# Dilated attention's output gate: SiLU made from Tanh on ScalarE and a product on VectorE

## The reference, cut to what matters

```python
def dilated_layer(x, c, kv_groups, ada_w, ada_b, norm_g, w_in, q_norm_g, w_out):
    h = rms_norm(x, norm_g) * (1 + scale) + shift
    qz = h @ w_in                                  # 3 x 8 query heads and z, 8 x 128 wide
    q = rms_norm(q, q_norm_g) * (HEAD_DIM ** -0.5)
    ...
    alpha = jax.nn.softmax(jnp.stack(lses), axis=0)
    o = jnp.sum(alpha[..., None] * jnp.stack(outs), axis=0).astype(x.dtype)
    y = o.reshape(bsz, s, B_WIDTH) * jax.nn.silu(z)
    return x + gate * (y @ w_out)
```

## Time and profile before

| | |
|---|---|
| median of 3 runs | 2087.05 us (2085.76 to 2090.64) |
| profiled execution | 2079.87 us |
| its span, first to last instruction | 2078.2 us |
| TensorE busy | 1920.6 us, 92% |
| VectorE busy | 1135.0 us, 55% |
| ScalarE busy | 777.8 us, 37% |
| mean granted TensorE clock | 0.965 of full speed |
| stage qz | about 518 to 826 us |

### The profile page before, as it was taken

The page is one execution under the profiler, slowest core; times in us unless marked ns, Lnnn a source line. Parts: engine busy times, 40 slices in busy tenths (PEclk is TensorE's granted clock), DMA queues, the critical chain, the costliest instruction groups (busy, mean ns, idle before and its releaser), DMA issues.

```text
span 2078.2 us, 23372 instructions
## 1 busy us (share of the span) xinstructions
PE 1920.6 (92%) x8572; PEld 1542.5 (74%) x8572; DVE 1135.0 (55%) x1554; ACT 777.8 (37%) x999; POOL 39.3 (2%) x96
## 2 busy tenths in 40 slices
PE   5999999989999996999999987999996979999997
PEld 4788888867788884778888864776654758888885
DVE  6346565477366665554334556598645464433455
ACT  3455553243455554322323233224344342222232
POOL 1000000000000000000000000000000000000000
PEclk8999999989999998999999998999998999999997
DMA  8445655412222210233233241241211223334321
GB/s 306 154 122 176 179 169 158 136 61 81 61 61 61 61 61 21 81 101 96 78 110 101 71 111 41 86 116 42 61 41 52 90 58 85 90 91 121 87 73 63
DMA packets 288194, 198.41 MB, mean 95 GB/s; under 512 B 6562, under 2 KB 275188, under 8 KB 287092
## 3 DMA queue, kind: packets, MB, share of 16 engines
q1 hardware_dynamic: 279568, 163.63, 27.4%
q0 software_dynamic: 8064, 33.56, 4.6%
q10 hardware_dynamic: 484, 0.16, 0.0%
HBM read 195.21 MB, written 2.11 MB: 95 GB/s over the span
## 4 chain that ended last, share of the span: by engine, by line
PE 84%; DVE 8%; ACT 3%; issue 3%; DMA 1%; DVEq 0%; POOL 0%; ACTq 0%; POOLq 0%
PE acc L575 20%; PE acc L577 20%; PE acc L576 20%; PE acc L765 3%; PE acc L767 3%; PE acc L766 3%; PE acc L989 1%; DVE s_rstd L1497 1%; DMA s_ada_w<-in_a_ada_w 1%; PE ob L815 1%; PE acc L991 1%; PE acc L990 1%; ACT s_w_high L1047 1%; PE ob L831 1%; PE sc L949 1%
## 5 line engine op out<-in xcount | busy, mean ns | idle before, releaser
L1459 DVE TENSOR_TENSOR s_w_low<-s_raw,s_w_high 128x2048 fp32r<-128x2048 f32 x159 | 364.5, 2292 | 351.9 <-ACT s_w_high L1047 351.8
L575 PE MATMUL acc<-s_h_high,s_w_high 128*128 128x512 f32 x1248 | 494.4, 396 | 31.6 <-DVE s_h_low L1860 11.7
L576 PE MATMUL acc<-s_h_low,s_w_high 128*128 128x512 f32 x1248 | 487.7, 391 | 0.0
L577 PE MATMUL acc<-s_h_high,s_w_low 128*128 128x512 f32 x1248 | 487.5, 391 | 0.0
L1047 ACT ACTIVATE s_w_high<-s_raw 128x2048 fp32r<-128x2048 f32 x159 | 303.0, 1906 | 23.8 <-PE sc L660 17.9
L575 PEld LDWEIGHTS acc<-s_h_high,s_w_high 128*128 128x128 f32 x1248 | 235.3, 189 | 89.9 <-issue 35.7
L575 PE MATMUL acc<-s_b_high,s_w_high 128*128 128x512 f32 x640 | 255.9, 400 | 30.7 <-DVE s_branch L2051 15.6
L577 PEld LDWEIGHTS acc<-s_h_high,s_w_low 128*128 128x128 f32 x1248 | 235.4, 189 | 49.4
L576 PEld LDWEIGHTS acc<-s_h_low,s_w_high 128*128 128x128 f32 x1248 | 235.4, 189 | 49.2 <-issue 2.0
L576 PE MATMUL acc<-s_b_low,s_w_high 128*128 128x512 f32 x640 | 252.0, 394 | 0.0
L577 PE MATMUL acc<-s_b_high,s_w_low 128*128 128x512 f32 x640 | 251.7, 393 | 0.0
(11 more groups left out here) (290 smaller groups left out, 2188.3 us busy)
## 6 DMA issues: line engine op xcount, KB each, us to landing
s_raw<-in_a_w_in SPq DMA_DIRECT2D x48, 512.0 KB, 5.0
s_raw<-in_ffn_w_gate SPq DMA_DIRECT2D x44, 512.0 KB, 4.0
s_raw<-in_ffn_w_up SPq DMA_DIRECT2D x44, 512.0 KB, 5.2
s_raw<-in_w_in SPq DMA_DIRECT2D x36, 512.0 KB, 4.2
s_raw<-in_b_w_in SPq DMA_DIRECT2D x32, 512.0 KB, 5.2
s_ada_w<-in_b_ada_w POOLq DMA_DIRECT2D x24, 512.0 KB, 5.0
s_raw<-in_ffn_w_down SPq DMA_DIRECT2D x32, 384.0 KB, 3.9
s_raw<-in_ffn_w_down SPq DMA_DIRECT2D x32, 320.0 KB, 3.7
```

What stands on the lines that cost most here:

```text
L575: pe.matmul(acc[b][:, :], w_high[:, o:o + P], hi, start=(k == 0), stop=False, skip_group_check=grouped)
L576: pe.matmul(acc[b][:, :], w_high[:, o:o + P], lo, start=False, stop=False, skip_group_check=grouped)
L577: mm = pe.matmul(acc[b][:, :], w_low[:, o:o + P], hi, start=False, stop=(k == nk - 1), skip_group_check=grouped)
L1459: dve.tensor_tensor(w_low[:, w], raw[:, w], w_high[:, w].bitcast(F32), ALU.subtract).then_inc(w_ready, 1)
```

## The change

ScalarE no longer applies Silu to z but Tanh with a scale of 0.5, still from the bank into zb. It no longer releases the bank; it counts a new semaphore `z_tanh`. VectorE waits for it and makes (zb + 1) * acc[1] into zb, which is z (1 + tanh(z/2)), twice the SiLU, and then releases the bank. This product, `gate_silu(s - 1)`, stands in step s at n = 0 behind `tops` and ahead of the low part of the weights. `output` waits for the product too. yb holds twice the wanted values until it is split; both parts are halved there, in the Copy by its scale and in VectorE's instruction, which becomes a scalar_tensor_tensor.

```diff
-                    act.activation(zb[j][:, :], acc[1][:, :], ACT.Silu).then_inc(evac[1], 1)
+                    act.activation(zb[j][:, :], acc[1][:, :], ACT.Tanh, scale=0.5).then_inc(z_tanh, 1)
...
             for k in range(KD):
-                high_of(yb[:, k * T:(k + 1) * T], h_high, k, o_taken, k + 1, h_high_ready)
+                act.wait_ge(o_taken, k + 1)
+                act.activation(h_high[:, k * T:(k + 1) * T], yb[:, k * T:(k + 1) * T], ACT.Copy, scale=0.5).then_inc(h_high_ready, 1)
...
+            def gate_silu(a):
+
+                dve.wait_ge(z_tanh, a + 1)
+                dve.scalar_tensor_tensor(out=zb[a % 2][:, :], in0=zb[a % 2][:, :], scalar=1.0, in1=acc[1][:, :],
+                                         op0=ALU.add, op1=ALU.mult).then_inc(evac[1], 1)
+
             def output(a):
 
+                dve.wait_ge(evac[1], t0 // 2 + 2 * a + 2)
                 dve.wait_ge(pv_ready, a + 1)
...
+                    if s > 0 and n == 0:
+                        gate_silu(s - 1)
                     if s < NQ and n % 2 == 0:
                         next_low(s + q0, n // 2)
             scale(NQ - 1, 3)
             output(NQ - 1)
             for k in range(KD):
-                low_of(yb[:, k * T:(k + 1) * T], h_high, h_low, k, h_high_ready, 3 * KD + k + 1, h_ready)
+                dve.wait_ge(h_high_ready, 3 * KD + k + 1)
+                dve.scalar_tensor_tensor(out=h_low[:, k * T:(k + 1) * T], in0=yb[:, k * T:(k + 1) * T], scalar=0.5,
+                                         in1=h_high[:, k * T:(k + 1) * T].bitcast(F32), op0=ALU.mult, op1=ALU.subtract)\
+                   .then_inc(h_ready, 1)
```

More of the change, by code:

```diff
@@ L301, in build @@
         qsq_summed, qms_ready, q_root = sem("qsq_summed"), sem("qms_ready"), sem("q_root")
-        qr_ready = sem("qr_ready")
+        qr_ready, z_tanh = sem("qr_ready"), sem("z_tanh")
         silu_ready, hid32_ready = sem("silu_ready"), sem("hid32_ready")
```

## The result

| | before | changed |
|---|---|---|
| median of 20 runs | 2085.06 us (2077.72 to 2091.81) | 2090.05 us (2086.64 to 2094.20) |
| ratio | | 1.0027, interval 1.0017 to 1.0037 |
| profiled execution | 2079.87 us | 2092.94 us |
| its span | 2078.2 us | 2091.0 us |
| ScalarE busy | 777.8 us | 757.5 us |

The change makes the kernel slower by 5 to 5.6 us, although it takes 20.3 us of work from ScalarE.

What follows compares the result with a forecast made beforehand. TensorE, busy 92% of the span, was taken to bound the kernel. Heads 2 to 6 +5.2, s = 1 +0.1, last head -0.2, end +0.1, clock +1.8: +7.0 us on the median 2087.05, 2094.0 us; range 2088.5 to 2101 us.

Steps and rivals of the forecast that it cites:

- What bounds, and what the loads are worth: Steady heads: TensorE bounds; two table loads go, 2.57 us of ScalarE a head, shortening a head by only 0.35 us.
- The wait behind `tops`: TensorE before `q_half(s, 1, 0)`: idle some 2.0 us for VectorE's product; the wait before L831 vanishes; net +1.04 us a head.
- Later slack: Rest of a head after the new wait: only TensorE is late, so the +1.04 us a head stays.
- the heads s = 1 and 2: s = 1 costs about 0.1 us, its 2.34 us idle time absorbing the delay; s = 2 pays 1.04 us.
- The last head: End of the stage: the Silu load on the chain goes, 1.28 us against 1.04 us of lateness: -0.2 us.
- Halving `yb`: Split of `yb` at the end: eight low parts become SCALAR_TENSOR_TENSOR, 748 against 683 ns, under 0.1 us showing.
- The clock: TensorE after the new idle time: one more spell of lower granted clock, +1.8 us; bounds none and seven (+12.6 us).
- The sum: Whole kernel: +5.2 us without the clock, +7.0 us with it, laid on the median 2087.05 us: 2094.0 us.
- the loads did not stay: Rival on ScalarE: Tanh read from another table than Exp, so the loads stay; 8.5 us, 2097.4 us with one spell; chance 0.05.
- The product was not done in time: Rival at `q_half(s, 1, 0)`: VectorE's product done within 2.85 us, no wait, 3.0 us gained, 2084.0 us; chance 0.05.

Runs made afterwards that it cites:

- the loads alone: Changed kernel without VectorE's product; ScalarE's Tanh releases the bank as Silu did: 2074.13 us, 0.9934 of the kernel before.
- The wait alone: Kernel before, with Silu and all loads, but the bank released by a VectorE product behind `tops` into a spare tile: 2094.53 us, ratio 1.0029.
- the product twice: Changed kernel with VectorE's product made twice, the first into a spare tile: 2094.43 us, 1.0028 of the kernel before.
- the second group: Runs on another chip: the changed kernel again without edit, three kernels with the column sums spread, and the kernel before, median 2085.05 us.
- The second profile of the changed kernel: Changed kernel run again without edit, with a profile of its own: 2089.60 us, 1.0015 of the kernel before.
- the sums spread: Changed kernel with TensorE's column sums of squares in three places instead of one stretch: 2090.98 us; same edit on the kernel before: 2088.31 us.
- the waits filled with products: Changed kernel with nine unneeded TensorE products ahead of the wait for VectorE's product: 2088.33 us; with the column sums also in three places: 2084.38 us.
- the padded kernel: Changed kernel with VectorE's product ahead of `tops`, plus two unneeded 128x384 TensorE products a head before the column sums: 2087.07 us, ratio 1.0017.
- the copy ahead: Product ahead of `tops`, plus ScalarE's copy of the last row block's transposed probabilities before the next head's query copy and squares: 2093.24 us, 1.0037.

## Why the prediction was right

**What bounds, and what the loads are worth**: right. Both loads left the steady heads; the bias came earlier and the scores released `tops` in its place, 0.35 us for 2.57 us of ScalarE, as the heads of 34.08 us with the loads alone show (34.07 by the steps). No run here showed the longer switch that the Trainium skill (ScalarE: Activation LUTs, "What ACT_TABLE_LOAD costs") gives; the loads that are left are 1.28 us each.

**The wait behind `tops`**: right in place and size. 2.09 us of idle time against "some 2.0", seven times, no wait left before L831, and +0.97 us a head against +1.04. The product took 0.69 us: I had taken 748 ns from an instruction of the same kind that reads the bank too, and the lower bound was the true value. That is not the difference, though, for the product started 0.19 us behind the last instruction of `tops` (662.15 to 662.34) where I had 0.08, and so the idle time came out a little longer than forecast. The head is shorter than by my sum because TensorE's way from L831 to the next head's L787 took 25.39 us instead of 25.57, of which 0.08 us lie in the sums. The wait alone (2.4 us; the expected delay of 2.62 us less the 0.25 us by which the records of L806 and L765 overlap where nothing waits) and the product twice (+0.60 us of wait) confirm the wait from two sides, and the product in front of `tops` takes it away.

**Later slack**: right in the steady heads, where nothing took the delay back. In the first part of the stage the step is not confirmed: the heads s = 1 and 2 cost 2.35 us together where I had 0.1 + 1.0, with two spells in either profile. TensorE's wait of 2.34 us in s = 1 did absorb the delay, but the sums of s = 1 then waited 0.7 us for ScalarE. What makes the other half microsecond was not separated. This term of the sum was 1.2 us too small.

**The last head**: right in direction. The bias came without the load; -0.6 us in the profile, less a spell whose size I can only take from others, against -1.3 us in that part by the steps. The second profile of the changed kernel has no spell behind those sums, and there the part takes 61.58 us against 62.39, which is -0.8. Halving `yb` cost what it was thought to: the wait ahead of the output weights' first product grew from 1.47 to 1.54 us.

**The clock**: the term was wrong in its make and, as far as the runs can tell, in its sign. I counted the spells of one profile of before as a fixed three, and added one for the new idle time. But the runs of before spread over 14 us; its profiled execution had few spells. The changed kernel's profiles show three and four spells in the five steady heads, mostly behind the old stretch of sums and not behind the new wait. In the second group the 35 runs of before have a mean granted clock of 0.9618 and the 12 of the changed kernel 0.9632. At 1.7 us for each 0.001 the clock took nothing and gave back some 2 us, an estimate that is uncertain by as much.

**The sum**: near for reasons that are in part luck. Measured are 5.0 to 5.6 us; the sum without the clock was 5.2, with it 7.0. But the parts of the profiles, without their spells, add up to 2.35 + 4.85 - 0.6 = 6.6 us and not to 5.2: the first part cost more and the last gave back less than I had. That the measured difference is smaller again is what a slightly higher clock in the changed kernel would make of it. The forecast of 2094.0 us is high by 4 us: 2.0 of these since the median of the three runs lay above that of the twenty, and 2.0 by the difference of 7.0 and 5.0.

**The rivals**: the loads did not stay. The product was not done in time, and the experiment in which it was shows that this rival was priced by the waits (3 us) and without the clock (some 10 us more).

The best kernel is the changed one with one call moved, the product ahead of `tops`: 2074.85 us, 0.9936 of the kernel before. Most of its gain rests on missing the lower clock, which 0.33 us of padding a head undid, and so may not outlast the next edit of the stage.

## What to carry to other kernels

Ask of each buffer not only who does the work, but who releases it and what stands ahead of that release on its engine: here 0.69 us of work moved to an engine with time to spare cost 2.09 us of waiting, and in front of one call instead of behind it, nothing. Work taken from an engine off the path is worth the wait that it ends, 0.35 of 2.57 us here. And where the runs of a kernel spread far more than its parts explain, compare the length of an undisturbed loop pass in the traces before the medians, and the granted clock of the runs beside them: a third of a microsecond in the pass moved the median by 10 us and more.

## What the runs showed of the hardware

- The spells of the lower clock in the steady heads follow a thin stretch of TensorE: an idle time of 2.1 us in some heads (five of six with the sums spread), of 1.9 us in four of six, of 2.7 us in all six, the 2.6 us of one-column products in some, these with 0.8 us of idle time ahead in all five. None was seen in heads whose longest idle time was 0.7 us and whose sums were spread, nor behind the waits filled with products. A spell makes a head 1.6 us longer; the spells of 6.8 us in the padded kernel and with the copy ahead make it 3.1 to 3.2 longer.
- The length of the idle time does not decide it alone. In s = 1 an idle time of 2.34 us (ahead of L801) has a spell within 0.8 us behind it in each of the seven profiles that hold it, among them that of before. The longer one that takes its place (ahead of L765), 2.43 us in four profiles and 3.04 us with the product twice, has none behind it in any of the five.
- How often they come changes with 0.33 us more in the pass, from none in the profile at 34.08 us to four in five at 34.4 with the same stretches (one in five in the profile of before, at 34.42). Whether the length itself does it, and why, stays open; that the clock is decided at moments which the kernel's loop doesn't set, and the heads drift against them, would fit this and the point above, but was only argued.
- The spread of the runs of before is the clock's: 2078.00 us at a mean granted clock of 0.967, 2093.34 us at 0.958.
- A 128x512 scalar_tensor_tensor with one operand in the bank took 687 ns, and the one that halves and subtracts 683 ns, as the plain two-operand forms do (692 and 683 ns), while the residual's, with a column as its scalar, takes 748.
